# Loading the experts' gate and up weights over 128 partitions, with x1 stored in a permuted column order to match

## The reference

```python
mix = hybrid_mixer(x, w_in, b_in, conv_w, mh_norm_g, w_out)    # mLSTM heads | gated conv, @ w_out
x1  = layer_norm(ALPHA * x + mix, ln_mix_g, ln_mix_b)
# router: softmax(x1 @ router_w + router_b); the best of 4 groups of experts, and the top 2 in it
# expert e on the rows routed to it:
hdn = silu(xb @ w_gate[e]) * (xb @ w_up[e])                    # w_gate[e], w_up[e]: 1024 x 512
y   = hdn @ w_down[e]                                          # w_down[e]: 512 x 1024
out = layer_norm(ALPHA * x1 + sum_of(gate * y), ln_moe_g, ln_moe_b)
```

## Time and profile before

| | |
|---|---|
| median of 3 runs | 1752.69 us (1748.73 to 1753.18) |
| the profiled execution | 1745.88 us, with a span of 1744.4 us |
| mean granted TensorE clock | 0.954 of full speed |
| mixer block | 0 to about 951 us |
| first expert matmul | 980.09 us |
| last matmul of the last expert's U tile | about 1712.5 us |

### The profile page before, as it was taken

One profiled execution on the slowest core, in us unless ns is written; L12 is line 12 of the kernel. 1 busy time (PEld: TensorE's weight loads), 2 busy tenths in 40 slices (PEclk: granted clock), 3 DMA queues, 4 the chain that ended last, 5 costly groups with the idle time before them and its releaser, 6 DMA issues. The chain is left out here.

```text
span 1744.4 us, 24141 instructions
## 1 busy us (share of the span) xinstructions
PE 1578.2 (90%) x9060; PEld 1369.9 (79%) x9060; DVE 1121.4 (64%) x1859; ACT 659.8 (38%) x904; POOL 435.8 (25%) x366
## 2 busy tenths in 40 slices
PE   8999999999999999999995599998878888888884
PEld 6888888888888888888884588897867788887873
DVE  4546867558666576855777666665656575756656
ACT  3234324244241443423424244344443443444442
POOL 2100134000160000610000433343443335142433
PEclk9999999999999999999998799998989899898987
DMA  7422535323363224342256398988997979888972
GB/s 232 145 75 83 182 109 182 97 73 108 135 216 97 75 97 156 134 152 91 73 159 203 89 211 198 210 189 202 213 235 181 222 165 254 178 223 186 217 205 84
DMA packets 121909, 276.26 MB, mean 158 GB/s; under 512 B 18192, under 2 KB 20368, under 8 KB 121280
## 3 DMA queue, kind: packets, MB, share of 16 engines
q1 hardware_dynamic: 93568, 187.64, 40.3%
q0 software_dynamic: 27648, 84.96, 17.5%
q10 hardware_dynamic: 576, 2.10, 0.3%
HBM read 229.66 MB, written 48.40 MB: 159 GB/s over the span
## 5 line engine op out<-in xcount | busy, mean ns | idle before, releaser
L1284 PE MATMUL mix_acc<-kept_xT,mix_w_high 128*128 128x512 f32 x640 | 256.9, 401 | 2.9 <-DVE mix_w_low L1093 2.9
L2329 PE MATMUL moe_gate_psum<-moe_xT_high,moe_gate_up_high 128*128 128x288 f32 x512 | 160.1, 313 | 109.5 <-DVE moe_gate_up_low L1943 76.4
L1943 DVE TENSOR_TENSOR moe_gate_up_low<-kept_w_gate_up_raw,moe_gate_up_high 128x2048 fp32r<-128x2048 f32 x64 | 146.5, 2289 | 169.7 <-ACT moe_gate_up_high L1799 136.1
L1286 PE MATMUL mix_acc<-kept_xT,mix_w_low 128*128 128x512 f32 x640 | 251.2, 393 | 0.0
L1285 PE MATMUL mix_acc<-kept_xT,mix_w_high 128*128 128x512 f32 x640 | 250.3, 391 | 0.0
L1681 POOL DMA_INDIRECT moe_x_quarter_rows<-x,kept_places x144 | 155.5, 1080 | 366.2 <-DVE moe_xT_low L1977 262.4
L937 DVE TENSOR_TENSOR mix_w_low<-mix_w_raw,mix_w_high 128x2048 fp32r<-128x2048 f32 x71 | 164.6, 2319 | 105.9 <-ACT mix_w_high L750 105.7
L750 ACT ACTIVATE mix_w_high<-mix_w_raw 128x2048 fp32r<-128x2048 f32 x71 | 135.9, 1915 | 233.5 <-PE mix_acc L1286 233.5
L2329 PEld LDWEIGHTS moe_gate_psum<-moe_xT_high,moe_gate_up_high 128*128 128x128 f32 x512 | 102.6, 200 | 117.6 <-DVE moe_gate_up_low L1943 81.7
L1799 ACT ACTIVATE moe_gate_up_high<-kept_w_gate_up_raw 128x2048 fp32r<-128x2048 f32 x64 | 121.9, 1907 | 122.0 <-issue 64.2
L2331 PE MATMUL moe_gate_psum<-moe_xT_high,moe_gate_up_low 128*128 128x288 f32 x512 | 157.0, 307 | 0.2 <-issue 0.2
(11 more groups left out here) (473 smaller groups left out, 3359.6 us busy)
## 6 DMA issues: line engine op xcount, KB each, us to landing
mix_w_raw<-in_w_in SPq DMA_DIRECT2D x56, 1024.0 KB, 5.3
kept_w_gate_up_raw<-in_w_gate SPq DMA_DIRECT2D x64, 512.0 KB
kept_w_gate_up_raw<-in_w_up SPq DMA_DIRECT2D x64, 512.0 KB
queries_keys_or_down_raw<-in_w_down SPq DMA_DIRECT2D x32, 1024.0 KB
mix_w_raw<-in_w_out SPq DMA_DIRECT2D x16, 1024.0 KB, 5.1
kept_conv_or_residual<-in_x POOLq DMA_DIRECT2D x16, 512.0 KB, 5.8
mix_x_rows<-in_x POOLq DMA_DIRECT2D x12, 512.0 KB, 4.3
x<-kept_conv_or_residual POOLq DMA_DIRECT2D x12, 512.0 KB, 2.9
```

The source lines that it names most:

```text
L1284: pe.matmul(out, ah, bh, start=first, stop=False)
L1286: return pe.matmul(out, al, bh, start=False, stop=last)
L1943: return dve.tensor_tensor(wl[:, n % RING].rearrange("p c k n -> p k c n"), raw_gu[:, :, :, f * P:(f + 1) * P], wh[:, n % RING].rearrange( ...
L2329: pe.matmul(out, ah, bh, start=first, stop=False)
```

## The change

1. `load_gate_up` reads the weights in their natural order, row c*128+p to partition p: four transfers of 1 MB, each over 128 partitions, in place of eight of 512 KB, each over 32 partitions. The bytes are the same. ACT's wait counts 64 in place of 128 for each expert.
2. So that the turned rows meet these weights, x1 is stored with its columns in another order: feature b*128+j*32+d is put at j*256+b*32+d. In the loop POOL does the four bias additions in a row, then permutes each tile with a `tensor_copy` from `R` into `XN[t % 2]` and stores that. A copy from the third on waits until the store before last from the same half of `XN` has landed; the wait for all four stores ahead of the multiplications by alpha is gone. SP waits for all x1 stores of the group before, ahead of its broadcast into `XN` at stage 5.
3. In the last group ACT makes the four permuted copies, into a buffer that lies over `yT`, and after them its alpha copies; SP stores the copies.
4. `LISTLO` and `LISTCOL` become fp32r (a tensor laid over the same memory). The list matmuls of expert 3 move from behind block f=1 to behind f=0, and DVE makes the tables ahead of `split_dn` of expert 3.

```diff
@@ mixer: the store's new order, SP's wait at stage 5, SP's last stores
+        def by_chunks(rows):
+            return rows.rearrange("p (b j d) -> p b j d", b=KC, j=STRIPS)
+        def by_quarters(rows):
+            return rows.rearrange("p (j b d) -> p b j d", b=KC, j=STRIPS)
...
                     if stage == 5:
                         sp.wait_ge(zero_out, 4 * 16)
                         sp.sem_inc(sp_idle, 1)
+                        for stored in x1_out:
+                            sp.wait_ge(stored, g * (NT // 2 * 16))
+                            sp.sem_inc(sp_idle, 1)
...
-                sp.wait_ge(v.x1_ready, (NG - 1) * NT + t + 1)
+                sp.wait_ge(late_quarters, t + 1)
                 row = (NG - 1) * GT + t * P
-                sp.dma_start(x1_dram[row:row + P], R[:, t]).then_inc(keep.late_x1, 16)
+                sp.dma_start(x1_dram[row:row + P], late_rows[:, t]).then_inc(keep.late_x1, 16)
@@ mixer: POOL, end of a group in the loop
                     pool.tensor_tensor(R[:, t], R[:, t], lnb[:], ALU.add).then_inc(v.x1_ready, 1)
+                wait_apart(pool, pool_idle, xt_ps, g * NT + 2 * NT)
+                for t in range(NT):
                     wait_apart(pool, pool_idle, v.x1_ready, g * NT + t + 1)
+                    if t >= 2:
+                        wait_apart(pool, pool_idle, x1_out[t % 2], g * (NT // 2 * 16) + 16)
+                    own.step(pool.tensor_copy(by_quarters(XN[:, t % 2]), by_chunks(R[:, t])))
+                    wait_apart(pool, pool_idle, *own.due(g))
                     row = g * GT + t * P
-                    pool.dma_start(x1_dram[bass.ds(row, P)], R[:, t]).then_inc(x1_out, 16)
-                wait_apart(pool, pool_idle, x1_out, (g + 1) * NT * 16)
+                    pool.dma_start(x1_dram[bass.ds(row, P)], XN[:, t % 2]).then_inc(x1_out[t % 2], 16)
@@ mixer: ACT, last group
+                    act.wait_ge(acc_full, NG * FULL)
+                    for t in range(NT):
+                        act.wait_ge(v.x1_ready, g * NT + t + 1)
+                        act.activation(by_quarters(late_rows[:, t]), by_chunks(R[:, t]), ACT.Copy)\
+                           .then_inc(late_quarters, 1)
@@ load_gate_up
-    quarter = w_gate.shape[0] // STRIPS
+    half = keep.raw_gu.shape[2] // 2
     for k, w in enumerate((w_gate, w_up)):
-        for j in range(STRIPS):
-            rows = w[j * quarter:(j + 1) * quarter].rearrange("(b d) n -> d b n", d=TW)
-            engine.dma_start(keep.raw_gu[j * TW:(j + 1) * TW, k], rows).then_inc(keep.gu_in, 16)
+        src = w.rearrange("(c p) n -> p c n", p=P)
+        for q in range(2):
+            c = slice(q * half, (q + 1) * half)
+            engine.dma_start(keep.raw_gu[:, k, c], src[:, c]).then_inc(keep.gu_in, 16)
@@ experts: ACT's wait, DVE's order, PE's order
-                act.wait_ge(gu_in, r * (NE * 128) + (e + 1) * 128)
+                act.wait_ge(gu_in, r * (NE * 64) + (e + 1) * 64)
...
-                    split_dn(r, e)
                     if e == 3:
                         lists(r)
+                    split_dn(r, e)
...
-                        if e == 3 and f == 1:
+                        if e == 3 and f == 0:
```

More of the change, by code:

```diff
@@ L430, in mixer @@
         wh, wl = (sb(n, [P, 2, KH, BANK], F32R) for n in ("w_high", "w_low"))
+        with nc.sbuf_tensor("mix_late_x1_by_quarters", [P, NT, D], F32) as late_rows:
+            pass
         yTh, yTl = (sb(n, [P, KC, GT], F32R) for n in ("yT_high", "yT_low"))
@@ L576, in mixer @@
         ln_done = sem("ln_normalised")
-        x1_out, xa_out = sem("x1_stored"), sem("alpha_x1_stored")
+        x1_out = [sem(f"x1_stored{k}") for k in range(2)]
+        xa_out, late_quarters = sem("alpha_x1_stored"), sem("late_x1_by_quarters")
         dve_own = sem("dve_own")
@@ L666, in _ @@
             for t in range(NT):
-                sp.wait_ge(v.x1_ready, (NG - 1) * NT + t + 1)
+                sp.wait_ge(late_quarters, t + 1)
                 row = (NG - 1) * GT + t * P
-                sp.dma_start(x1_dram[row:row + P], R[:, t]).then_inc(keep.late_x1, 16)
-        POOL_TURN = NT
+                sp.dma_start(x1_dram[row:row + P], late_rows[:, t]).then_inc(keep.late_x1, 16)
+        POOL_TURN = 2 * NT
         @block.gpsimd
@@ L730, in _ @@
             loads(NG - 1, True)
-            for stored in (x1_out, xa_out):
-                pool.wait_ge(stored, (NG - 1) * NT * 16)
+            for stored, of in ((x1_out[0], NT // 2), (x1_out[1], NT // 2), (xa_out, NT)):
+                pool.wait_ge(stored, (NG - 1) * of * 16)
                 pool.sem_inc(pool_idle, 1)
@@ L1574, in experts @@
         free = keep.conv_or_residual
-        LISTLO = free[:, 0:TILES * P].rearrange("p (t s) -> p t s", s=P)
-        LISTCOL = free[:, TILES * P:TILES * (P + NLIST)].rearrange("p (t c) -> p t c", c=NLIST)
+        list_tables = keep.list_tables
+        LISTLO = list_tables[:, 0:TILES * P].rearrange("p (t s) -> p t s", s=P)
+        LISTCOL = list_tables[:, TILES * P:TILES * (P + NLIST)].rearrange("p (t c) -> p t c", c=NLIST)
         small2 = free[:, TILES * (P + NLIST):RTILES * D]
@@ L2105, in list_one_hots @@
                                          at.unsqueeze(2).to_broadcast([P, TILES, NLIST]), ALU.is_equal))
-                    do(dve.tensor_tensor(LISTCOL, LISTCOL, keep.tokp1[:].unsqueeze(2).to_broadcast([P, TILES, NLIST]),
+                    do(dve.tensor_tensor(LISTCOL, LISTCOL.bitcast(F32), keep.tokp1[:].unsqueeze(2).to_broadcast([P, TILES, NLIST]),
                                          ALU.mult))
@@ L2438, in hybrid_layer @@
         keep.ident = sb("identity", [P, P])
+        with nc.sbuf_tensor("kept_list_tables", [P, 4 * (2 * BANK + 2)], F32R) as keep.list_tables:
+            pass
         keep.conv_or_residual = sb("conv_or_residual", [P, 4 * (2 * BANK + 2)])
```

## The result

| | before | changed |
|---|---|---|
| four runs, median (from, to) | 1752.44 us (1748.73 to 1753.18) | 1651.72 us (1648.90 to 1663.44) |
| profiled execution, span | 1744.4 us | 1649.4 us |
| first expert matmul | 980.09 us | 984.82 us |
| first matmul of the last expert | 1676.93 us | 1585.50 us |
| mean granted TensorE clock | 0.954 | 0.976 |

The ratio is 0.9442, with a 95% interval of 0.9395 to 0.9489: 5.6% faster. The forecast was 1648 us. Measured twice more beside the experiments, the same kernel stood at 0.9381 (0.9359 to 0.9403) and 0.9387 (0.9368 to 0.9406), with medians of 1639.3 and 1639.75 us against 1747.42 and 1746.96.

A forecast was written before the change was run, and what follows sets the result against it. PE was taken to wait in the experts for late gate/up loads, slow through their transfers' shape. 1745.9 - 109.8 + 9 = 1645 us against the profiled execution, 1648 with half the runs' median offset; range 1628 to 1692.

The forecast's parts named there:

- The bound and the load: Experts: PE waits for late gate/up loads; over 128 partitions a load takes 13.5 us, 16.1 with list rows.
- a sign that it is wrong: Gate/up loads: the prediction counts as wrong if a load still takes over 18 us.
- The experts: First fifteen experts: bound by PE at 39.0 us each, 588.2 us in all instead of 696.9.
- what is not hidden: Ten experts: half a margin, 0.9 us, lost in each to DVE's or ACT's order, +9 us; bounds 0 and 36.
- the 1.1 for the clock: First expert: 1.1 us more because it starts at a low clock.
- The last expert: Last expert: it no longer follows a gap, 1.1 us less.
- The lists: List matmuls of expert 3: one pass in place of two, 2.1 us instead of 4.3.
- The copies in the loop: Mixer loop: twelve permuted POOL copies of 3.4 us each, price 0 as long as one takes under 8.0 us.
- the sum would grow by nothing, since both have room: Mixer: POOL's copies and DVE's low splits may lengthen each other, at a cost of 0 us.
- the 1 us that the forecast allowed: Start of the experts: first expert matmul within 1 us of 980.09; a late start would mean the prediction is wrong.
- The rooms of 3.7 and 15 us: Mixer loop: slack for the copies' stores, 3.7 us ahead of SP's broadcast and 15 more at the weight load behind.
- the third case: Gate/up loads: rival that the rate comes out near 300 GB/s, 1675 to 1695 us, chance 0.10.

The follow-up runs named there:

- second profile: Profile of after_again, the changed kernel itself run once more, unaltered: 0.9381 of the kernel before, median 1639.3 us.
- third profile: Profile of after_third, the changed kernel itself run a third time, unaltered: 0.9387 of the kernel before, median 1639.75 us.
- first_half: Changed kernel with gate/up loads cut by columns, left half first, a semaphore per half, so block 0 waits for 2 MB: 1627.94 us, 0.9322.
- two_adds: Changed kernel with POOL's bias additions in the loop made in pairs, each pair followed by its permuted copies and stores: 0.9397 of the kernel before.

## Why the prediction was right, step by step

- **The bound and the load.** Right. The load was what PE waited for, and the shape of the transfer set its rate: 197 to 211 GB/s onto 32 or 64 partitions, 337 to 398 onto 128. The forecast load without other transfers, 13.5 us, was 14.6 in expert 0 (issued at 1000.04, landed at 1014.61). Beside others the sum took 2.6 us for list rows; it needed 5 to 9. The scatters, and their additions in DRAM, were left out of it. The forecast named a load of over 18 us as a sign that it is wrong; from issue to ACT's split eight loads of the second profile are at 18.2 to 22.4. They cost little, since each is at most 2.1 us late for PE.
- **The experts.** 588.2 us and 9 for what is not hidden were forecast, 597. The three profiles of the changed kernel had 600.7, 590.3 and 587.1. Both terms were off and partly made up for one another. An expert bound by PE takes 38.2 us and not the 39.0 read from expert 4 before, in which PE was idle for 0.4 us and busy for 0.4 more: 11.4 us less over fifteen. What is not hidden, the 9 and the 1.1 for the clock, 10.1 together, was 25.3 in the first profile, with the holes, 14.9 in the second and 11.7 in the third. In the last two, 9.7 and 9.0 us of it are waits for the low split, and most of the rest is the stretch at half clock that the first expert begins with.
- **The last expert.** 3.5 us less, forecast 1.1; in the third profile it is 1.5.
- **The lists.** 16 passes in 1.9 us of PE against 4.3, forecast 2.1. By periods, 1.8 us of expert 3.
- **The copies in the loop.** Oversized and harmless: 1.04 us each, not 3.4, near the MEMSET row and not the multiplications. SP's broadcast came at 515.80 in place of 512.85, and nothing waited for it.
- **The mixer.** The step that failed is "the sum would grow by nothing, since both have room". The first expert started 4.7 us later, outside the 1 us that the forecast allowed, and this too it had named as a sign of being wrong. The first low split of a group has no room, PE stands ready for it. The Trainium skill had it, in "SBUF — State Buffer", section "Who interferes with whom": two SBUF inputs on DVE contend with a reading POOL operation, and whoever issues first keeps the pair. The trace agrees, with 3.76 us for the split and 4.44 for the addition behind it. The rule was quoted, but for the copies; the change's effect was on the additions, which it had only put closer together. By the starts of DVE's low splits, the three ends of groups cost 1.5, 1.1 and 1.4 us, in the first profile as in the second; 2.9 of these 4.0 us are PE's waits for the first low split. That is nearly all of the 4.1 us of the second profile. The first had started 0.6 us sooner and lost 1.3 more in the routing of the last group, where the granted clock was 0.57 from 938 to 942 us and 1.00 in the kernel before from 935 to 939. The third profile has this fall of the clock too and the second has not. Why it falls there was not tried.
- **The last group's copies on ACT.** 3.88 us; ACT's idle time ahead of the experts went from 5.62 to 1.85 us. Hidden, as forecast.
- **Two slips in the sums.** The rooms of 3.7 and 15 us for the copies add up to 18.7 and not 18.5, and the range that is said to take in the third case ends at 1692, below that case's 1695. Neither changes the outcome.

Against the profiled execution the forecast was 1645.1 us and the time 1650.9. The errors are 4.7 us for the mixer, 15.2 more that was not hidden, 11.4 less for an expert bound by PE, 0.3 less in the lists and 2.4 less in the last expert; together 5.8. So 1651.7 against 1648 is a right mechanism with a right size of its main term, and in the other terms it is luck: errors of up to 15 us happened to offset one another. The same kernel at 1639.3 us lies 8.7 below the forecast.

## What to carry to other kernels

Read the rate of a transfer in a stretch where nothing else moves, beside its partitions: a full DMA share says nothing about how much a full engine moves, and only transfers over all 128 partitions moved 1.7 to 2 times as much. When a load is late by one or two microseconds, don't only make it faster; let the first consumer wait for its own part of it (first_half, 12 us for a change of a few lines). And when operations are put in a row on POOL, look for the DVE operation with two inputs in SBUF that used to slip in between.

## What the runs showed of the hardware that was not expected

- A 2 KB packet of the gate/up load took 165 to 170 ns on average onto 32 or 64 partitions and 91 to 95 onto 128, and the DMA share was near 1 with either.
- A GpSimd copy of 128 x 1024 through runs of 32 elements took 1.04 us (median of twelve), the plain bias addition of that size 2.4 to 3.7 in the kernel before and the multiplication in place 2.8 to 4.8. A MEMSET of the size took 0.95, so the permutation can cost little; a copy without it was not run.
- A DVE operation of 0.67 us took 5.51 behind two POOL additions and a copy in a row (two_adds): it did not get in between them. In the changed kernel DVE's split, begun during the third of four additions in a row, did get in ahead of the fourth. What decides between the two, no run tells.
- The y scatters with addition in DRAM slow the transfers beside them: over whole loads 279 to 310 GB/s with it, 292 to 338 without.
- Two sets of runs of one program differed by 0.6% in their ratio to the kernel before, and in the profiles most of the difference lies in holes of 0.2 to 0.9 us between matmuls of one block, and in what follows them.
